# Constant matmuls, regrouped recurrence outputs and late value products in the attention stage of a two-block transformer kernel

## What is computed

```
h = _rms_norm(x, mix_norm[layer])
proj = h @ w_in[layer]
aq, ak, av, hq, hf, hi, hg = jnp.split(proj, split_at, axis=-1)
...
attn_out = _dilated_attention(aq, ak, av)      # 8 heads of 64 columns, causal windows
rec = _hgrn2(hq, hf, hi, lower_bounds[layer])  # 4 heads of 128 columns, chunks of 64 tokens
rec = _rms_norm(rec, hg_out_norm[layer]) * jax.nn.silu(hg)
mixed = jnp.concatenate([attn_out, rec], axis=-1)
x = x + mixed @ w_out[layer]
```

## Time and profile before

| | us |
|---|---|
| median of 3 runs | 1333.2 |
| lowest and highest of them | 1331.91, 1340.69 |
| the profiled execution's own time | 1335.28 |
| its span in the trace | 1333.4 |
| PE busy in it | 1269.5 |
| DVE, ACT, POOL busy | 612.2, 466.9, 205.6 |

### The profile page before, as it was taken

The page is one execution under the profiler, slowest core; times in us unless marked ns, Lnnn a source line. Parts: engine busy times, 40 slices in busy tenths (PEclk is TensorE's granted clock), DMA queues, the critical chain, the costliest instruction groups (busy, mean ns, idle before and its releaser), DMA issues.

```text
span 1333.4 us, 18498 instructions
## 1 busy us (share of the span) xinstructions
PE 1269.5 (95%) x7906; PEld 924.0 (69%) x7906; DVE 612.2 (46%) x816; ACT 466.9 (35%) x634; POOL 205.6 (15%) x207
## 2 busy tenths in 40 slices
PE   6999999998999999999899999997999899999995
PEld 6999997886799999888664444434898665444432
DVE  6644556845676764476731111117465651111114
ACT  5544344655446444325410101014676420001111
POOL 0000000410499990030000000000033000000000
PEclk9999999999999999989999999998999999999998
DMA  9555553540555555515599999996523399999992
GB/s 390 185 180 180 186 190 129 191 159 28 174 185 187 190 189 167 190 41 188 200 373 419 422 421 420 421 421 248 169 92 127 127 350 395 421 421 421 421 420 113
DMA packets 47750, 338.33 MB, mean 254 GB/s; under 512 B 5296, under 2 KB 5296, under 8 KB 7728
## 3 DMA queue, kind: packets, MB, share of 16 engines
q1 hardware_dynamic: 45936, 330.53, 64.6%
q10 hardware_dynamic: 1728, 6.55, 1.3%
HBM read 336.02 MB, written 1.05 MB: 253 GB/s over the span
## 4 chain that ended last, share of the span: by engine, by line
PE 89%; DVE 7%; ACT 2%; issue 1%; DMA 1%; SPq 0%; ACTq 0%; DVEq 0%
PE pb L178 88%; DVE halves L307 1%; DVE SM L1476 1%; DVE Xs L1487 1%; DMA ring<-in_ffn_w 1%; PE pb L1916 1%; DVE Xs L403 0%; DVE Xs L1482 0%; DVE Xs L405 0%; DVE XN L340 0%; ACT halves L299 0%; DVE p L1655 0%; DVE XN L349 0%; DVE Xs L1500 0%; DVE XTl L392 0%
## 5 line engine op out<-in xcount | busy, mean ns | idle before, releaser
L178 PE MATMUL pb<-XTh,halves 128*128 128x256 f32 x1856 | 338.8, 283 | 6.9 <-DVE XTl L392 4.9
L307 DVE TENSOR_TENSOR halves<-ring,halves 128x2048 fp32r<-128x2048 f32 (+1 forms) x122 | 285.1, 2352 | 130.2 <-ACT halves L299 129.9
L178 PEld LDWEIGHTS pb<-XTh,halves 128*128 128x128 f32 x1856 | 291.2, 192 | 9.1 <-issue 4.1
L178 PE MATMUL pb<-XTl,halves 128*128 128x256 f32 x928 | 262.3, 283 | 0.0
L299 ACT CAST halves<-ring 128x2048 fp32r<-128x2048 f32 (+1 forms) x122 | 227.4, 1874 | 83.4 <-PE pb L178 79.4
L178 PE MATMUL pb<-ring,gather 128*64 128x512 f32 x832 | 189.8, 598 | 3.2 <-DVE gather L2054 1.7
L178 PEld LDWEIGHTS pb<-XTl,halves 128*128 128x128 f32 x928 | 177.8, 192 | 0.9
L178 PE MATMUL pb<-halves,XTh 128*128 128x512 f32 x512 | 160.5, 395 | 5.0 <-DVE halves L307 3.0
L178 PEld LDWEIGHTS pb<-ring,gather 128*64 128x64 f32 x832 | 57.5, 137 | 109.2 <-issue 105.0
L2050 DVE TENSOR_TENSOR slots_h<-slots_silu,pb 128x256 f32<-128x256 f32 x32 | 13.5, 421 | 229.3 <-ACT slots_silu L2012 229.3
L178 PEld LDWEIGHTS pb<-halves,XTh 128*128 128x128 f32 x512 | 95.6, 190 | 26.0 <-DVE halves L307 6.0
(11 more groups left out here) (348 smaller groups left out, 1389.4 us busy)
## 6 DMA issues: line engine op xcount, KB each, us to landing
ring<-in_moe_w SPq DMA_DIRECT2D x144, 1024.0 KB, 13.6
ring<-in_ffn_w SPq DMA_DIRECT2D x66, 1024.0 KB, 5.0
extra<-in_moe_w SPq DMA_DIRECT2D x48, 1024.0 KB, 14.6
ring<-in_w_tok SPq DMA_DIRECT2D x10, 1024.0 KB, 5.0
ring<-in_ple_gate SPq DMA_DIRECT2D x8, 1024.0 KB, 4.9
ring<-in_w_out SPq DMA_DIRECT2D x4, 1024.0 KB, 4.9
ring<-in_ab_out SPq DMA_DIRECT2D x4, 1024.0 KB, 4.9
ring<-in_sb_v SPq DMA_DIRECT2D x4, 1024.0 KB, 22.8
```

Of the source, the lines that this page charges most:

```text
L178: return e.matmul(out, l, r, start=start, stop=stop, **kw)
L307: e.tensor_tensor(l, raw_of(n), h.bitcast(F32), ALU.subtract).then_inc(*low.mark(n))
```

## The change

Four things change, all in the attention stage of the first block's mixer.

1. In steps 2 and 3 PE runs one more matmul ahead of `pe_turn_p`: the identity with 512 columns of constants, written to bank 7, where nobody reads it before the value products overwrite it.
2. `pe_rec_out` runs the four 128\*128 matmuls of a half first and its 128\*64 matmuls after them. Only the first of a bank now carries the start flag.
3. `squares` is parted: `squares(0)` stands in ACT's step 4, ahead of turned_p(2), and `squares(1)` in step 8, behind turned_p(6). `means` moves from DVE's step 7 to 9, `roots` from ACT's step 8 to 10 and `gated` from DVE's step 9 to 10.
4. The loop of PE ends a step earlier, and `pe_pv(6)` and `pe_pv(7)` run behind group 0 of the output projection. That group now waits, bank by bank, until DVE has read the last scores (banks 2 and 3) and ACT the last transposed probabilities (banks 4 and 5).

```
--- before.py
+++ after.py
@@ -667,7 +667,9 @@
                 e.wait_ge(*state_n.at(2 if tt else 1))
                 for h in range(4):
                     hv = slice(h * 128, h * 128 + 128)
-                    i = mm(e, P[:, hv], att8[:, 2 * h + tt, :], HI3[:, tt, hv], True, False, skip_group_check=True)
+                    mm(e, P[:, hv], att8[:, 2 * h + tt, :], HI3[:, tt, hv], h == 0, False, skip_group_check=True)
+                for h in range(4):
+                    hv = slice(h * 128, h * 128 + 128)
                     for c in (2 * tt, 2 * tt + 1):
                         if c:
                             i = mm(e, P[(c % 2) * 64:(c % 2) * 64 + 64, hv], E1h[:, h, c * 64:c * 64 + 64],
@@ -746,19 +748,23 @@
             pe_qk_turn(e, 0)
             e.wait_ge(*qk_norm.at(0, 1))
             pe_tok(e, ("w_tok", 2), 4, 5, between=lambda: (pe_rec_state(e, 0), pe_qk_turn(e, 1)))
-            for i in range(11):
+            for i in range(10):
                 if i < 8:
                     pe_scores(e, i)
                 if i < 2:
                     pe_rec_state(e, 1 + i)
                 elif i == 4:
                     pe_rec_out(e)
+                if i in (2, 3):
+                    mm(e, banks[7][:, :], ident, CO[:, 0:512], True, True)
                 if 2 <= i <= 9:
                     pe_turn_p(e, i - 2)
-                if i >= 3:
+                if 3 <= i < 9:
                     pe_pv(e, i - 3)
             e.wait_ge(*mix_low.at("pv", 1))
-            pe_down(e, "w_out", XT3, range(1), 2)
+            pe_down(e, "w_out", XT3, range(1), 2, free=lambda b: att_max.at(6 + b) if b < 2 else pt_kept.at(4 + b))
+            pe_pv(e, 6)
+            pe_pv(e, 7)
             pe_rec_turn(e)
             e.wait_ge(*mix_low.at("pv", 3))
             pe_down(e, "w_out", XT3, range(1, 2), 2)
@@ -824,14 +830,13 @@
                 e.wait_ge(*att_masked.at(h))
                 e.copy(ksT[:, h * 256:h * 256 + 256], banks[h % 2][:, 256:512]).then_inc(*ks_kept.mark(h))
 
-            def squares():
-                for tt in range(2):
-                    e.wait_ge(*rec_out.at(tt))
-                    for h in range(4):
-                        hv = slice(h * 128, h * 128 + 128)
-                        i = e.activation(XN3[:, tt, hv], banks[1 - tt][:, hv], ACT.Square,
-                                         accum_out=rss[:, 4 * tt + h:4 * tt + h + 1])
-                i.then_inc(*rec_sq.mark())
+            def squares(tt):
+                e.wait_ge(*rec_out.at(tt))
+                for h in range(4):
+                    hv = slice(h * 128, h * 128 + 128)
+                    i = e.activation(XN3[:, tt, hv], banks[1 - tt][:, hv], ACT.Square,
+                                     accum_out=rss[:, 4 * tt + h:4 * tt + h + 1])
+                i.then_inc(*rec_sq.mark(tt))
 
             def roots():
                 e.wait_ge(*rec_mean.at())
@@ -859,13 +864,15 @@
             for i in range(12):
                 if i < 8:
                     exps(i)
+                if i == 4:
+                    squares(0)
                 if 2 <= i <= 9:
                     turned_p(i - 2)
                 if i >= 5 and i % 2:
                     values((i - 5) // 2)
-                if i == 6:
-                    squares()
-                elif i == 8:
+                if i == 8:
+                    squares(1)
+                elif i == 10:
                     roots()
             act_split(e, c, last_tok + SPLIT)
             rec_xt()
@@ -958,7 +965,7 @@
                 i.then_inc(*state_n.mark(n))
 
             def means():
-                e.wait_ge(*rec_sq.at())
+                e.wait_ge(*rec_sq.at(1))
                 e.tensor_scalar(rss, rss, 1.0 / 128, 1e-6, ALU.mult, ALU.add).then_inc(*rec_mean.mark())
 
             def gated():
@@ -994,9 +1001,9 @@
                     values((i - 5) // 2)
                 if i in (1, 2):
                     states(i)
-                elif i == 7:
+                elif i == 9:
                     means()
-                elif i == 9:
+                elif i == 10:
                     gated()
             dve_split(e, c, last_tok + SPLIT)
             rec_xt()
```

2 lines of the change are left out of this document (1 added, 1 removed).

## The result

| | before | after |
|---|---|---|
| median, us | 1340.2 (15 runs) | 1328.22 (15 runs) |
| lowest and highest | 1331.23, 1343.51 | 1326.14, 1334.24 |
| ratio of after to before | | 0.9922 (95%: 0.9902 to 0.9942) |
| profiled execution, span | 1333.4 | 1330.1 |
| first scores to first addition (L403) in it | 298.13 to 347.44 | 298.08 to 342.68 |

The 15 runs of before include the three known ahead of the prediction. Nine of them lie at 1340 us or above, five between 1331 and 1334. The median 1333.2 of the first three belonged to the lower group; after has no run above 1334.24. By the ratio the change saves 0.8%, about 10 us (the medians differ by 12.0), while the attention stage of the two profiles differs by 4.7 us. The rest of this text is about both numbers.

A forecast was written before the change was run, and what follows sets the result against it. PE was taken to bound the kernel, busy for 1269.5 of 1333.4 us. Terms of 2.0 + 1.7 + 0.7 = 4.4 us, off the median 1333.2, gave 1328.8 us, range 1325 to 1334.5.

The forecast's parts named there:

- Term 1: Recurrence's outputs on PE: grouping matmuls by shape saves 2.0 us, or 1.2 if the 128*64 ones stop running side by side.
- rival of unhidden weight loads: Recurrence's outputs: records start a weight load apart, so grouping gains 0.3 us instead of 2.0; time 1330.5; chance 0.08.
- Term 2: PE's 1.88 us wait ahead of pv(5): moving the squares lets ACT copy head 5 earlier, gaining 1.7 us.
- term 3: From pv(5) through the output projection: late value products gain 0.7 us, mostly clock; about 0 or -1.0 if it falls.
- Sum: All three terms, 4.4 us in the attention stage, taken to reach the end whole: 1328.8 us, 0.33% faster; chance 0.50.
- The covers: Slack before PE would wait: 2.3 us for `gated` at the recurrence's transposes, half a microsecond at group 2.
- a gain lost to the clock behind the stage: Case: first addition at 343 but span not 4 us shorter; then low clock after the stage took the gain.
- By the same rows they gain nothing either: the clock was 1.00 there without them.: Constant matmuls in PE's idle times of 1.01 and 0.85 us: gain 0, cost 0 to 0.2 us.
- rival "slower": Low clock in three or more further stretches (5.1 us) outweighs the 4.4 us gain: 1333.9 us; chance 0.07.
- chance of 0.01 for a gain of over 1%: Over 1% needs 13 us from a stage with under 3 us of idle time and 6.3 of regrouped matmuls.

The follow-up runs named there:

- e7: The changed kernel without the grouping by shape (constants, parted squares and late values in): median 1331.9 us, ratio to before 0.9966, stage 46.62 us.
- e1: The kernel before with only the two constant matmuls added: median 1333.7 us, ratio to before 0.9985, stage 49.26 us.
- e5: The kernel before with only the value products of heads 6 and 7 moved behind group 0: median 1340.5 us, ratio to before 1.0000, stage 58.59 us.
- e6: The kernel before, unchanged, run for one more profile: 1340.5 us (1 run), stage 59.13 us.
- e10: The kernel before with the constant matmuls and the late value products, squares as before: 1332.6 us (1 run), stage 49.78 us.
- e11: The changed kernel with two more constant matmuls in the state-space mixer's input products: median 1327.7 us, ratio to before 0.9921, stage 44.62 us.
- e3: The kernel before with only the recurrence's outputs grouped by shape: median 1334.2 us, ratio to before 0.9962, stage 52.03 us.
- e2: The changed kernel without the constant matmuls: median 1330.5 us, ratio to before 0.9936, stage 48.83 us.
- e8: The changed kernel with constant matmuls of 64 instead of 512 columns, same places: median 1328.1 us, ratio to before 0.9932, stage 48.60 us.

## Why the prediction was right, and where not

The time (1328.8 against 1328.22) and the range held, the time in part by luck, as the last point says. The single steps:

- **Term 1**, 2.0 us: 2.02 (e7 against after). The two 128\*64 matmuls of a head still run side by side. The price of 0.17 us for a change of shape carried over. The rival of unhidden weight loads would have given 0.3. The Trainium skill, "TensorE: Matmul & The Clock Gate", Part 3 on packing small matmuls, says that a weight load overlaps matmuls in flight only when its row group differs; the trace disagrees with it here, with the 20 matmuls in 4.22 us and not in 6.0.
- **Term 2**, 1.7 us, and **term 3**, 0.7 us: 2.64 together (e1 to e7, 49.26 to 46.62), of which the squares bring 2.37 and the late values 0.27 on top. Term 3 was mostly clock, as said, but that clock comes with the squares, which take the idle time away. By themselves the late values gave 0.54 at half clock (e5 against e6) and lost 0.52 where the clock fell under group 0 (e10 against e1), each read from single executions.
- **Sum**: 4.71 us in the stage (49.31 to 44.60), 4.4 predicted; group 0 of the output projection starts 6.1 us earlier (327.12 to 320.99), 5.8 counted, and the first addition stands at 342.68 against "near 343.0". The covers held: `gated` ended at 325.98 (323.82 + 2.16), 1.75 us ahead of the transposes, 2.3 counted. Group 2 did not wait, since PE is busy without a break from 325 to 345 us; L986, the last thing it needs, ended at 333.66. Timeline of DVE after:

```profile
323.82 2.16 DVE L978 SCALAR_TENSOR_TENSOR XN<-pb,SM,p 128x128 f32<-128x128 f32 x8
...
332.26 1.40 DVE L986 SCALAR_TENSOR_TENSOR XTl<-pb,PR,XTh 128x512 fp32r<-128x512 f32 x2
```

- **The span** shrank by only 3.3 us. The prediction named this case, a gain lost to the clock behind the stage: from the first addition to the end before took 986.0 us and after 987.4. Over all profiled executions this rest lies between 981.1 (e5) and 989.6 (e1), with the same instructions but for the two matmuls that e11 adds, and the low clock in it between 27.0 us (e11) and 50.0 (e1), 28.1 in e5. Between before and after it is not the amount of low clock that differs (42.9 and 42.5 us) but the places: after is 7.8 us ahead at 613 us, behind before's long stretch near 565, and loses most of that again where it has stretches of its own or longer ones, near 690 and 1100. What each of them cost was not measured.
- **The step that failed** is "By the same rows they gain nothing either: the clock was 1.00 there without them." It took the granted clock of one execution for the kernel's. In about half of the executions (19 of 35, by their mean clocks; one of them seen in a trace) the clock very probably falls there, and in that trace the stage is 59.1 us long, not 49.3; after is 14.5 us shorter than that. The grouping's worth in those executions (7.1 us, e6 to e3) and that of the constants (4.2, e2 to after) are both missing from the sum. The base of the sum failed in the same way: 1333.2 was the median of three runs out of two groups, 1340.69 beside 1331.91 and 1333.2, and was taken for the typical time. The forecast time came out right because it started from the lower group, which is what the change leaves. That is luck: from the median of the fifteen runs, 1340.2, the same sum gives 1335.8, above the top of the range. As a difference the forecast, 0.33%, was too small: 0.78% was measured, and its interval does not hold 0.33%. The rival "slower" had even pointed at the spread of 8.8 us, and read it as something the change could make worse only. The chance of 0.01 for a gain of over 1% rested on this too, and on a misreading: the idle times of the stage are 1.01 + 0.85 + 1.88 = 3.74 us, not under 3.

Left open: why the alternating matmuls kept the clock at half for 30 us while the grouped ones had it back in 10. PE was busy in both. It is also open what decides whether the clock falls: the first profile of before and e6 reach the stage at the same time (298.13 and 298.19) with the same idle times of 1.01 and 0.85 us, and the clock falls in only one of them. How much of the 0.8% is the constants' and how much the grouping's can't be told from medians: e2 and e7, each with one of the two missing, are at 0.9936 and 0.9966, and their intervals overlap.

## What to carry to other kernels

Where runs of one kernel fall into two groups, look at the mean granted clock of the runs and take a second profile ahead of pricing anything: a filler matmul in an idle time is worth nothing in one execution and several us in the next. In this kernel the short idle times ahead of a long run of small matmuls were the ones to fill, with matmuls long enough to fill them. Group small matmuls by array shape, for what each change of shape costs and for the clock, which came back sooner in the grouped order. Take the idle time away before moving dense work up behind it.

## What the runs showed of the hardware

- The granted clock can stay at 1.2 GHz through 30 us in which PE is never idle: from 304.3 to 334 us in e6, small matmuls in changing shapes. The Trainium skill, "TensorE: Matmul & The Clock Gate", Part 1 on the clock gate, ties a throttled clock to idling; here the low clock outlasted it by far.
- Idle times of 1.01 and 0.85 us, 1.4 us apart, came with a fall of the clock in five of six profiled executions, and so did what 64 columns left of them in e8 (0.65 and 0.23 us). None of the seven in which they were filled had it. The idle time of 1.9 us ahead of pv(5) was followed by a fall in all four profiles that have it (before, e1, e3, e10).
- In the same stage PE's busy time is 45.35 us of 49.31 at a mean clock of 0.97 (before), 57.09 of 59.13 at 0.74 (e6) and 43.70 of 44.60 at 1.00 (after): that PE is busy does not show that it runs at full clock.
- A change between the shapes 128\*128 and 128\*64 costs about 0.17 us at full clock, an estimate from 6.27 us with 16 changes and 4.22 with 4. Two 128\*64 matmuls on different halves of a bank's partitions run side by side: the half of the outputs with eight of them takes 3.15 us, the one with four 3.12.
